# A norm's first tile walked chunk by chunk, its squares summed on TensorE and VectorE, and gate rows spread by DMA

## The reference, cut to what matters

```python
def rmsnorm(x, g):
    y = x * rsqrt(mean(x * x, axis=-1) + EPS) * g
for layer in range(2):
    xn = rmsnorm(h, norm_mix)
    h = h + mixer(xn)                  # layer 0: gated DeltaNet (4 heads) + retention (4 heads); layer 1: mLSTM (4 heads)
    hidden = relu(rmsnorm(h, norm_ffn) @ w_up)
    h = h + (hidden * hidden) @ w_down
y = rmsnorm(h, final_gain)
```

## Time and profile before

| | |
|---|---|
| median of 3 runs | 2977.67 us (2976.99 to 2977.9) |
| the profiled execution's own time | 2978.46 us |
| its span, first to last instruction | 2976.7 us |
| mean granted clock of TensorE | 0.974 |
| busy: PE, DVE, POOL, ACT | 2837.4, 1562.2, 790.5, 354.0 us |

### The profile page before, as it was taken

How to read it: one execution, slowest core, us unless ns; L and a number is a source line. 1 busy time by engine, 2 the same in 40 slices (tenths; PEclk the granted TensorE clock), 3 DMA queues, 4 the chain that set the end, 5 groups by cost and what they waited for, 6 DMA issues and landing times.

```text
span 2976.7 us, 43441 instructions
## 1 busy us (share of the span) xinstructions
PE 2837.4 (95%) x17818; PEld 2718.5 (91%) x17818; DVE 1562.2 (52%) x2644; ACT 354.0 (12%) x598; POOL 790.5 (27%) x638
## 2 busy tenths in 40 slices
PE   7998988989999999999999999998989999999997
PEld 6888777889898999999999999997889999999997
DVE  6757658555667427154277435446476245172553
ACT  4212213121231000000001111112130000000001
POOL 5211111122223333333333212122212323232331
PEclk8999999999999999999999999999899999999999
DMA  2100101111121111111112112012221111111111
GB/s 109 43 23 22 37 15 37 51 44 51 51 103 40 47 48 45 50 43 50 43 50 94 50 50 59 29 59 66 80 50 43 43 51 43 51 43 50 48 45 71
DMA packets 42691, 151.10 MB, mean 51 GB/s; under 512 B 5768, under 2 KB 7688, under 8 KB 41488
## 3 DMA queue, kind: packets, MB, share of 16 engines
q1 hardware_dynamic: 30528, 111.20, 11.5%
q10 hardware_dynamic: 11984, 37.22, 3.4%
HBM read 130.32 MB, written 18.08 MB: 50 GB/s over the span
## 4 chain that ended last, share of the span: by engine, by line
PE 73%; DVE 5%; issue 3%; POOL 1%; ACT 1%; DMA 0%; DVEq 0%; ACTq 0%; POOLq 0%; SPq 0%
PE proj L374 65%; PE bank L420 6%; PE bank L407 1%; DVE ssq L740 1%; DVE x_lo L736 0%; PE bank L417 0%; PE bank L401 0%; POOL w_lo L303 0%; DVE x_lo L792 0%; DVE s L904 0%; PE bank L626 0%; DVE h L1372 0%; DVE s L750 0%; DVE s L903 0%; DVE s L812 0%
## 5 line engine op out<-in xcount | busy, mean ns | idle before, releaser
L374 PE MATMUL proj<-x_hi,w_hi 128*128 128x344 f32 x4788 | 1576.9, 329 | 46.4 <-DVE s L750 20.1
L374 PE MATMUL proj<-x_lo,w_hi 128*128 128x344 f32 x4788 | 1542.0, 322 | 0.0
L374 PE MATMUL proj<-x_hi,w_lo 128*128 128x344 f32 x4788 | 1541.3, 322 | 0.0
L374 PEld LDWEIGHTS proj<-x_hi,w_hi 128*128 128x128 f32 x4788 | 912.2, 191 | 76.9 <-issue 41.6
L374 PEld LDWEIGHTS proj<-x_lo,w_hi 128*128 128x128 f32 x4788 | 912.5, 191 | 2.7 <-issue 1.0
L374 PEld LDWEIGHTS proj<-x_hi,w_lo 128*128 128x128 f32 x4788 | 911.5, 190 | 0.0
L300 POOL TENSOR_TENSOR pool_gate<-pool_gate 1x1 f32<-1x1 f32 x204 | 50.9, 250 | 2131.5 <-PE proj L374 2117.0
L303 POOL TENSOR_TENSOR w_lo<-w_raw,w_hi 128x1024 fp32r<-128x1024 f32 x202 | 512.7, 2538 | 16.2
L1235 DVE TENSOR_TENSOR h<-h,proj 128x344 f32<-128x344 f32 x144 | 73.9, 513 | 446.2 <-PE proj L374 446.2
L1221 DVE TENSOR_TENSOR mlp_t<-proj,rbc 128x344 f32<-128x344 f32 x192 | 98.8, 515 | 227.1 <-PE proj L374 227.1
L301 POOL CAST w_hi<-w_raw 128x1024 fp32r<-128x1024 f32 x202 | 208.1, 1030 | 0.0
(11 more groups left out here) (268 smaller groups left out, 1897.1 us busy)
## 6 DMA issues: line engine op xcount, KB each, us to landing
w_raw<-w_all SPq DMA_DIRECT2D x204, 512.0 KB, 3.4
h<-x SPq DMA_DIRECT2D x8, 516.0 KB, 9.3
h<-x ACTq DMA_DIRECT2D x8, 516.0 KB, 6.4
h_spill<-h ACTq DMA_DIRECT2D x8, 516.0 KB, 2.7
h<-h_spill ACTq DMA_DIRECT2D x8, 516.0 KB, 6.5
y<-h ACTq DMA_DIRECT2D x8, 516.0 KB
sample_C<-state_c ACTq DMA_DIRECT2D x4, 1024.0 KB, 5.2
s_state_c<-sample_C ACTq DMA_DIRECT2D x4, 1024.0 KB
```

The lines of the kernel that those rows point to most:

```text
L374: last = nc.tensor.matmul(PJ[:, tt, 0:TT], w[slot][:, k, :], x[:, k, tt * TT:(tt + 1) * TT], start=(at == 0 and j == 0), stop=(at == len(o ...
```

## The change

It has three parts. First, the tile that follows a norm is walked chunk by chunk, all three thirds of a chunk before the next chunk, and the norm's three matmuls stand ahead of the last chunk: for both MLPs' first tiles and for `T_GC`. The norm's factor is made and awaited third by third. To fit this, each MLP's first group is written out, and the loop has two turns. Second, in the first norm POOL adds no squares: two thirds are summed over chunks and partitions by TensorE, one more matmul for each chunk and third, and DVE adds the third one. The halving of `vec` moves behind that stage. Third, the gate rows are written to DRAM (`rows_a`, `rows_c`, one DMA each), and each head's rows are loaded back with a DMA that reads one row 128 times; in mLSTM heads two loads of 8 columns stand in for the two small matmuls. The matmuls of `over_partitions` for gates, and the copies out of their banks, go.

```diff
@@ Pool
             for t in range(2):
                 split(t, 0, None)

-            for c in range(1, KC):
-                for tt in range(NT):
-
-                    pool.wait_ge(sq_made, 3 * c + tt + 1)
-                    if c > 1:
-
-                        pool.wait_ge(ssq_added, 3 * (c - 2) + tt + 1)
-                    nc.gpsimd.tensor_tensor(third(SSQ, tt), third(SSQ, tt), third(SQT, tt), ALU.add).then_inc(ssq_added, 1)
...
@@ TensorE, first_tile: behind the matmuls of chunk k
+                    for tt in range(SQ_BY_PE):
+
+                        pe.wait_ge(sq_made, 3 * k + tt + 1)
+                        last = nc.tensor.matmul(MB[tt][:, 0:TT], ones, third((SSQ, SQT)[k % 2], tt),
+                                                start=(k == 0), stop=(k == KC - 1))
+                        if k == KC - 1:
+                            publish(last, tt)
+                        else:
+                            last.then_inc(sq_summed, 1)
+                for tt in range(SQ_BY_PE, NT):
+                    pe.wait_ge(ssq_added, (tt - SQ_BY_PE + 1) * (KC - 1))
+                    publish(nc.tensor.matmul(MB[tt][:, 0:TT], ones, third(SSQ, tt), start=True, stop=True), tt)
...
+            def tile_as_x_comes(t, X, ready, order, number):
+
+                hi, lo = X
+                pe.wait_ge(w_split, t + 1)
+                for at, k in enumerate(order):
+                    if at == KC - 1:
+                        norm_finish(number)
+                    for tt in range(NT):
+                        if at == 0:
+                            pe.wait_ge(proj_drained, 3 * t + tt - 2)
+                        pe.wait_ge(x_ready, ready + 3 * at + tt + 1)
+                        for j, (w, x) in enumerate(((w_hi, hi), (w_hi, lo), (w_lo, hi))):
+                            last = nc.tensor.matmul(PJ[:, tt, 0:TT], w[w_slot(t)][:, k, :], x[:, k, tt * TT:(tt + 1) * TT],
+                                                    start=(at == 0 and j == 0), stop=(at == KC - 1 and j == 2))
+                        if at == KC - 1:
+                            last.then_inc(proj_full, 1)
...
                 if delta:
-                    over_partitions(sel(32 + h, 36), rows_a[0:36, :], "act")
                     yield "start"
-                    over_partitions(sel(h, 36), rows_a[0:36, :], "dve")
...
             def mixer_c(s, h):
-                over_partitions(sel(h, 100), rows_c[0:100, :], "dve")
-                claim(3, "dve")
-                mm(MB[3][:, NB:2 * NB], sel(64 + h, 100), rows_c[0:100, SEQ:TOK])
-                publish(mm(MB[3][:, 0:NB], sel(96 + h, 100), rows_c[0:100, SEQ:TOK]), 3)
                 yield "start"
-                over_partitions(sel(32 + h, 100), rows_c[0:100, :], "act")
...
-            def mlp(t0, X, Y, ready, hid, order):
-                with n.loop(GROUPS - 1, {}) as g:
+            def mlp(t0, X, Y, ready, hid, order, number):
+                tile_as_x_comes(t0, X, ready, order, number)
+                for k in range(1, KC):
+                    tile(t0 + k, w_slot(t0 + k), X)
+                for k in range(KC):
+                    tile(t0 + 8 + k, w_slot(t0 + 8 + k), Y, hid if k == 0 else None)
+                with n.loop(GROUPS - 2, {}) as g:
...
-            norm_finish(0)
...
-            norm_finish(1)
-            mlp(T_MLP0, XB, XA, XR["xg1"], XR["hid0"], ORDER[0])
-            tile(T_GC, w_slot(T_GC), XB, XR["xg2"])
-            norm_finish(2)
+            mlp(T_MLP0, XB, XA, XR["xg1"], XR["hid0"], ORDER[0], 1)
+            tile_as_x_comes(T_GC, XB, XR["xg2"], IN_TURN, 2)
...
@@ VectorE, a delta head, then an mLSTM head
-                    for tt in range(NT):
-                        ps = take(tt)
-                        nc.vector.tensor_copy(third(s[7], tt), ps[:, 0:TT]).then_inc(*done(tt))
-                    n.settle()
+                    v.wait_ge(g_in, n.awaited(g_in, 16)[1])
...
+                    v.wait_ge(beta_in, n.awaited(beta_in, 16)[1])
                     tt_(s[14][:], s[5][:], s[8][:], ALU.mult).then_inc(*n.made(to_pe))
...
-                for tt in range(NT):
-                    ps = take(tt)
-                    nc.vector.tensor_copy(third(s[12], tt), ps[:, 0:TT]).then_inc(*done(tt))
-                n.settle()
+                v.wait_ge(g_in, n.awaited(g_in, 16)[1])
                 for c in range(NC_):
-                    last = ts_(chunk(s[11], c), chunk(s[12], c), gcol[:, c, h:h + 1], 0.0, ALU.add, ALU.min)
-                ps = take(3)
-
-                nc.vector.tensor_copy(small[:, 10 * NB:11 * NB], ps[:, NB:2 * NB])
-                tt_(small[:, 8 * NB:9 * NB], ps[:, 0:NB], s[12][:, SEQ:TOK], ALU.add).then_inc(*done(3))
+                    ts_(chunk(s[11], c), chunk(grow, c), gcol[:, c, h:h + 1], 0.0, ALU.add, ALU.min)
+                v.wait_ge(cols_in, n.awaited(cols_in, 32)[1])
+                step(tt_(small[:, 8 * NB:9 * NB], small[:, 8 * NB:9 * NB], grow[:, SEQ:TOK], ALU.add))
...
@@ VectorE, before the first layer
             nc.vector.memset(eps[:, 0:1], EPS)
-            nc.vector.memset(eps[:, 1:2], 1.0)
+            nc.vector.memset(eps[:, 1:2], 1.0).then_inc(setup_done, 1)
             v.wait_ge(consts_in, 32)
-            for a, m in ((V_CONV, 48), (V_GDN, 4)):
-                last = ts_(vec[:, a:a + m], vec[:, a:a + m], 0.5, None, ALU.mult)
-            last.then_inc(setup_done, 1)
...
                     stt(lo, hh, gain, hi.bitcast(F32), ALU.mult, ALU.subtract).then_inc(x_ready, 1)
+                    if tt >= SQ_BY_PE and c:
+                        v.wait_ge(sq_made, 3 * c + tt + 1)
+                        tt_(third(SSQ, tt), third(SSQ, tt), third(SQT, tt), ALU.add).then_inc(ssq_added, 1)
...
@@ ScalarE
-                rsqrt_of_banks(rbc, 1.0 / D_MODEL, rbc_ready)
+                rsqrt_of_banks(rbc, 1.0 / D_MODEL, rbc_ready, by_third=True)
...
+            def row_to_all(rows, row, dst, landed):
+
+                a.dma_start(dst[:], io[rows][row:row + 1, :].broadcast_to([P, TOK])).then_inc(landed, 16)
...
             def mixer_ab(s, h, delta, start=None, midway=None):
                 a.wait_ge(*n.awaited(to_act))
+                if delta:
+                    row_to_all("rows_a", h, s[7], g_in)
+                    row_to_all("rows_a", 32 + h, s[8], beta_in)
...
-                if delta:
-                    for tt in range(NT):
-                        ps = take(tt)
-                        act(third(s[8], tt), ps[:, 0:TT], ACT.Copy).then_inc(*done(tt))
...
             def mixer_c(s, h, start=None, midway=None):
                 a.wait_ge(*n.awaited(to_act))
+                if h == 0:
+                    row_to_all("rows_c", h, grow, g_in)
+                row_to_all("rows_c", 32 + h, s[6], beta_in)
+                for row, j in ((96, 8), (64, 10)):
+                    a.dma_start(small[:, j * NB:(j + 1) * NB],
+                                io["rows_c"][row + h:row + h + 1, SEQ:TOK].broadcast_to([P, NB])).then_inc(cols_in, 16)
...
-                for tt in range(NT):
-                    ps = take(tt)
-                    act(third(s[6], tt), ps[:, 0:TT], ACT.Exp).then_inc(*done(tt))
-                n.settle()
-                tell(to_dve)
+                a.wait_ge(beta_in, n.awaited(beta_in, 16)[1])
+                act(s[6][:], s[6][:], ACT.Exp).then_inc(*n.made(to_dve))
+                if h < HEADS - 1:
+                    row_to_all("rows_c", h + 1, grow, g_in)
...
+            a.dma_start(io["rows_a"], rows_a[0:36, :]).then_inc(rows_out, 16)
...
+            a.dma_start(io["rows_c"], rows_c[0:100, :]).then_inc(rows_out, 16)
```

73 lines of the change are left out of this document (51 added, 22 removed).

## The result

| | before | after |
|---|---|---|
| median | 2977.78 us (2976.99 to 2979.7) | 2946.18 us (2939.01 to 2950.29) |
| the profiled execution's own time | 2978.46 us | 2946.81 us |
| its span | 2976.7 us | 2945.0 us |
| mean granted clock of TensorE | 0.974 | 0.974 |

The ratio is 0.989 (0.987 to 0.991): 31.6 us faster, where 48.8 were forecast. The time lies inside the range, near its upper end, and the sign was right; a third of the gain is missing. One thing is new: the executions of the kernel before lie within 2.7 us of one another (nine later ones within 5.6), those of the kernel after within 11.3.

A forecast was written before the change was run, and what follows sets the result against it. TensorE, in flight 95% of the span, was taken as the bound, with VectorE leading in the first stage and delta heads. Terms summed to 48.3 us off 2978.5, giving 2930.2, median forecast 2929, range 2918 to 2949.

The forecast's parts named there:

- First tile: First norm and first tile: earlier start and chunks of 2.65 us bring the next tile to 37.3, 10.4 us less.
- The rival of the half clock: TensorE stays at half clock through the first tile, next tile at 54.2 instead of 47.75; total 2946 us; chance 0.07.
- Norms 1 to 3: Both MLPs' norms and the one between: TensorE's idle waits and half-clock work go, gaining 6.6, 4.4 and 6.1 us.
- The rival of the tile that doesn't follow x: Something else before the MLP comes as late as the squares, so norms 1 to 3 give nothing; 2946 us; chance 0.07.
- 1.1 stays idle: Norms 1 to 3: waiting for the norm's factor, TensorE still idles 1.1 us after the norm's matmuls and last chunk.
- Delta heads: Gate rows off TensorE only lengthen its wait; VectorE's saved copies, 1.36 us in each of four heads, gain 5.4.
- the clock: Delta heads: TensorE's longer wait drops its clock, losing 2.5 us a head, 10 in all; 2939 us; chance 0.12.
- Slow loads: Broadcast row loads, 128 reads of one DRAM row, outlast about 7 us of cover; 3001 us at 16 us landing; chance 0.05.
- mLSTM heads: Gate matmuls off TensorE gain 3.85 us in heads two and three, 3.3 in the first, 2.5 in the fourth: 13.5.
- waits of VectorE for row loads: Sign in the profile after: VectorE waits named after the row loads would make the prediction wrong.
- Turns of the loops: Writing out a group takes one loop turn of two from each MLP, 2.1 us, or none if straight code costs it.
- End: At the kernel's end, three Exps cost 0.2 us more than one.

The follow-up runs named there:

- delta_warm: Changed kernel plus, in each delta head, twelve unread TensorE passes and three unread matmuls ahead of each of three waits; median 2934.63 us, ratio 0.9857.

## Why the prediction was right in sign and short in size

**First tile: 10.4 forecast, 11.4 measured.** The start is 0.77 earlier instead of 1.3: ScalarE begins at 7.69, when `vec` has landed, and in the trace of before it had landed by 7.12. The chunks make up for it: 2.45 each from the third on, where 2.65 was taken, with VectorE's x_lo at 0.57 as priced. The rival of the half clock fell with the window's 1.00.

**Norms 1 to 3: 6.6, 4.4 and 6.1 forecast, 4.9, 4.5 and 5.8 measured.** The rival of the tile that doesn't follow x fell. What norm 1 lacks is a wait I left out: the chunk-wise tile writes to all three banks at once, so it needs the last drain of the tile before, 1.34 at 898.08, and 0.44 and 0.64 stay at the next two tiles. Together 2.4 stay idle; the step that said "1.1 stays idle" counted only the factor. The sum also took 1.4 for the norm's matmuls where its rows give 3.81 - 1.90 = 1.9, an error of the other sign.

**Delta heads: 5.4 forecast, -1.0 measured. This step failed.** It said that TensorE's matmuls only lengthen a wait and that the copies shorten the path. Both are so, but the longer wait isn't free: I wrote the clock down as a rival, at a loss of 10 and a chance of 0.12, and 6.4 of it came. delta_warm shows it by its opposite. The argument against it, that the lower clock ends once TensorE works again, is true and beside the point: it comes back at later waits. The sentence cited there from the Trainium skill, "TensorE: Matmul & The Clock Gate", section "HAM oscillation", that each long wait throttles the array anew, is what the trace shows behind the wait of 7.92 us, with a first matmul of 0.62 and a clock of 0.82 over the 15.4 us that follow. It does not settle the transposes: they took 3.03 us behind a wait of 2.23 in after, and 1.97 behind the same wait before. The rival deserved more than one chance in eight.

**Slow loads, the rival on the slower side,** fell: the row loads of the delta heads land in 6.0 us at the median, by part 6 of the page, against a cover of 7.1 and an estimate of 4.7.

```profile
s<-rows_a ACTq DMA_DIRECT2D x8, 516.0 KB, 6.0
```

**mLSTM heads: 13.5 forecast, 11.9 measured.** Heads two and three gave 3.9 each for 3.85. The first lost 1.3 where 3.3 was to be won, since its row, whose load comes first in the head, wasn't there for 4.25 us, and the second issue took 1.32; in the sum I had priced that wait at 0.55. The fourth gave 5.4 for 2.5, of which some 3.2 is the wait for POOL that other executions of the same code have again. The size held by two errors of opposite sign, which is luck. The prediction had named waits of VectorE for row loads as a sign that it is wrong. They are there, 4.2 us for the forget-gate row and 6.3 for the small loads, but in the mLSTM heads alone.

**Turns of the loops: 2.1 forecast, -4.0 measured. This step failed most.** The seams that were written out gave 1.2 each, as priced. But I costed the turn that stays at nothing new. The diff makes TensorE's code longer (a group for each MLP) and so moves the loops' heads, and the price of a jump goes by their place; the second MLP's head came to lie at the end of a block, and that cost 6.5. No row of before could have shown this: its four turns take 1.2 at most.

**End, -0.2 forecast, some -1.7 measured.** The last norm's matmuls run at half clock in after, and not in before (PE's timeline, after, then before):

```profile
2926.12 3.40 PE L412 MATMUL bank<-ssq,consts 128*128 128x344 f32 x6 [1.82 <-DVE ssq L759]
```

```profile
2959.36 2.00 PE L401 MATMUL bank<-ssq,consts 128*128 128x344 f32 x6 [1.82 <-DVE ssq L740]
```

The wait is 1.82 in both. Of the thirteen executions in the table five lose 1.1 to 1.8 here and eight 0.1 to 0.2; what decides it stays open.

Together: +1.0 first tile, -6.4 delta heads, -1.7 norm 1, -6.1 turns, -1.6 mLSTM heads, -1.5 at the end, -0.1 for the small ones make -16.4, from 48.3 to 31.9; the table has 31.7. The range held, though its bounds were added up wrongly: the terms at their lower bounds give 14.3, so 2963 and not about 2955, at their upper 57.7, so 2920 and not 2917; the slow-loads rival's 2978 - 48 + 72 is 3002.
